# Block ends, store waits, weight fetch and scatter order in a one-core streaming encoder layer

## The reference

```
m = W_out( sigmoid(x Wg_a) * (StickBreak(x) W_oa) + sigmoid(x Wg_b) * (MLA(x) W_ob) )
h = LayerNorm(ALPHA * x + m)
y = LayerNorm(ALPHA * h + PEER(h))
```

## Time and profile before

| what | value |
| --- | --- |
| median of the 3 runs shown | 4035.32 us (4028.1 to 4043.04) |
| profiled execution, own time | 4035.91 us |
| its span (first to last instruction) | 4034.2 us |
| mean granted TensorE clock | 0.883 |
| PE busy | 3200.7 us, 79% of the span |
| DVE busy | 2572.0 us, 64% |
| POOL busy | 1534.7 us, 38% |
| ACT busy | 1130.9 us, 28% |
| DMA | 1097.71 MB, mean 272 GB/s |
| dense stage | from 2486.2 us to the end, 1548 us |

### The profile page before, as it was taken

The page is one execution under the profiler, slowest core; times in us unless marked ns, Lnnn a source line. Parts: engine busy times, 40 slices in busy tenths (PEclk is TensorE's granted clock), DMA queues, the critical chain, the costliest instruction groups (busy, mean ns, idle before and its releaser), DMA issues. The chain is left out here.

```text
span 4034.2 us, 36222 instructions
## 1 busy us (share of the span) xinstructions
PE 3200.7 (79%) x10354; PEld 1799.7 (45%) x10354; DVE 2572.0 (64%) x5114; ACT 1130.9 (28%) x3097; POOL 1534.7 (38%) x1184
## 2 busy tenths in 40 slices
PE   9968998476757679388676593889998999989977
PEld 5735654242534445254354252444444444444433
DVE  0112148685746766575774674688888888888884
ACT  0212122352422522354342331222222222222211
POOL 0000026562631136463654677633333333333330
PEclk9878999688778889698877796999999999999999
DMA  5634479645467889544546696999999999999994
GB/s 159 245 138 132 157 278 350 232 132 161 130 222 268 286 319 335 192 130 140 161 130 201 193 293 205 336 392 404 398 393 409 412 407 405 389 410 398 400 405 138
DMA packets 373897, 1097.71 MB, mean 272 GB/s; under 512 B 90272, under 2 KB 208192, under 8 KB 287552
## 3 DMA queue, kind: packets, MB, share of 16 engines
q0 software_dynamic: 165072, 751.05, 50.0%
q1 hardware_dynamic: 189040, 326.24, 23.1%
q10 hardware_dynamic: 19584, 18.10, 1.3%
HBM read 1031.16 MB, written 63.02 MB: 271 GB/s over the span
## 5 line engine op out<-in xcount | busy, mean ns | idle before, releaser
L417 POOL DMA_INDIRECT expert_rows<-in_experts,picked_index x640 | 771.1, 1205 | 1554.0 <-DVE ff_sum L572 1441.8
L560 DVE SCALAR_TENSOR_TENSOR expert_rows<-expert_rows,h_tile 128x1024 f32<-128x1024 f32 x672 | 820.2, 1220 | 308.1 <-DMA expert_rows<-in_experts,picked_index 276.1
L572 DVE SCALAR_TENSOR_TENSOR ff_sum<-expert_rows,coefficients,ff_sum 128x1024 f32<-128x1024 f32 x672 | 861.4, 1282 | 112.6 <-ACT coefficients L523 111.2
L1719 PE MATMUL dense_act_ps<-dense_hT,key_columns 128*128 128x384 f32 x2048 | 719.5, 508 | 178.8 <-DMA key_columns<-in_key_columns 98.0
L440 POOL DMA_INDIRECT gates_by_expert<-dense_gate,gate_address x384 | 649.9, 1692 | 202.1 <-issue 143.6
L1727 PE MATMUL dense_out_ps<-dense_value_rows,dense_weights 128*128 128x512 f32 x1536 | 688.2, 600 | 24.5 <-DVE dense_weights L1792 24.4
L1719 PEld LDWEIGHTS dense_act_ps<-dense_hT,key_columns 128*128 128x128 f32 x2048 | 398.8, 198 | 515.5 <-DMA key_columns<-in_key_columns 157.7
L809 PE MATMUL proj_ps<-xT,w_in_block 128*128 128x384 f32 (+1 forms) x1392 | 430.0, 473 | 71.7 <-DMA w_in_block<-in_w_in 31.6
L1727 PEld LDWEIGHTS dense_out_ps<-dense_value_rows,dense_weights 128*128 128x128 f32 x1536 | 294.6, 192 | 378.9 <-issue 319.2
L809 PEld LDWEIGHTS proj_ps<-xT,w_in_block 128*128 128x128 f32 x1392 | 271.5, 196 | 229.8 <-issue 44.5
L517 ACT ACTIVATE activated<-dots 128x1 f32<-128x1 f32 (+2 forms) x620 | 122.4, 197 | 733.1 <-DVE expert_rows L560 718.2
(11 more groups left out here) (181 smaller groups left out, 3383.3 us busy)
## 6 DMA issues: line engine op xcount, KB each, us to landing
key_columns<-in_key_columns SPq DMA_DIRECT2D x128, 512.0 KB, 11.3
dense_value_rows<-in_experts SPq DMA_DIRECT2D x128, 512.0 KB, 8.2
w_in_block<-in_w_in SPq DMA_DIRECT2D x20, 2048.0 KB, 12.6
gates_by_expert<-zeros POOLq DMA_DIRECT2D x12, 2048.0 KB, 33.7
wq_head<-in_peer_wq SPq DMA_DIRECT2D x24, 1024.0 KB, 6.7
dense_gates<-gates_by_expert SPq DMA_DIRECT2D x128, 192.0 KB, 9.6
w_out<-in_w_out SPq DMA_DIRECT2D x3, 4096.0 KB, 13.8
expert_rows<-in_experts,picked_index POOLq DMA_INDIRECT x640, 10.1
```

Source lines behind the costliest of these rows:

```text
L417: pool.indirect_dma_start(to, None, self.a["experts"], bass.IndirectOffsetOnAxis(ap=index[:, k:k + 1], axis=0)).then_inc(self.got[p % self ...
L560: dve.scalar_tensor_tensor(place, place, 1.0, self.h[n % 2][:], ALU.mult, ALU.mult, accum_out=self.dots[:, s % TOPK:s % TOPK + 1]).then_in ...
L572: dve.scalar_tensor_tensor(total, self.ring[:, p % self.RING, D:2 * D], self.coef[:, y % TOPK:y % TOPK + 1], total, ALU.mult, ALU.add).the ...
L1719: mm = nc.tensor.matmul(up[it % 2][:, 0:W], keys[it % KB][:, k, :], hTd[:, k, :], start=(k == 0), stop=(k == KC - 1))
```

## The change

Four things are changed.

1. All blocks but the dense one are opened with `nc.Block(no_gpsimd_drain=True)`: the barrier stays, POOL's DRAIN in front of it goes.
2. The waits for stores at the ends of stages go. Their semaphores now live as long as the program, and the wait stands where the data is read or the buffer is written again: SP waits for stored scores at the start of the next `project` and POOL before it loads a tile's scores; `stick_attend` gets an SP stream that waits for the stored keys and values, and its DVE waits for the stored gates before the first output copy; SP waits for the stored MLA keys at the end of `mla_attend`; SP and ACT wait for the stored h rows at the start of `score_experts`, SP for the dense h at its end; in the dense stage ACT waits for stored scores at the start and SP before the first dense gates.
3. `mla_attend` loads the `w_o` tiles of j = 0 and j = 1; the second ring place moves to 4 KB that are free in that stage. `merge` no longer loads those of j = 1.
4. `SHARES` gets a fifth column, the scatters that each stage may take, and other row counts; a scatter's credit is this number spread over the stage's events (at most 90 of them), at most 4 kept.

```diff
@@ Experts
-        ((1, "project"), 50, 1, 7), ((1, "stick"), 16, 4, 5), ((1, "mla_project"), 8, 1, 1), ((1, "mla"), 12, 4, 4),
-        ((1, "merge"), 10, 2, 1), ((1, "norm"), 9, 1, 1), ((1, "scores"), 24, 1, 5),
-        ((2, "project"), 52, 1, 5), ((2, "stick"), 24, 4, 5), ((2, "mla_project"), 9, 1, 2), ((2, "mla"), 20, 4, 4),
-        ((2, "merge"), 10, 2, 2), ((2, "norm"), 9, 1, 1), ((2, "scores"), 25, 1, 5),
-        ((3, "dense"), 1000, 1, 24),
+        ((1, "project"), 46, 1, 7, 10), ((1, "stick"), 18, 4, 5, 36), ((1, "mla_project"), 9, 1, 1, 14), ((1, "mla"), 12, 4, 4, 30),
+        ((1, "merge"), 11, 2, 1, 14), ((1, "norm"), 9, 1, 1, 12), ((1, "scores"), 24, 1, 5, 12),
+        ((2, "project"), 46, 1, 5, 26), ((2, "stick"), 26, 4, 5, 64), ((2, "mla_project"), 10, 1, 2, 30), ((2, "mla"), 22, 4, 4, 56),
+        ((2, "merge"), 11, 2, 2, 24), ((2, "norm"), 11, 1, 1, 20), ((2, "scores"), 23, 1, 5, 20),
+        ((3, "dense"), 1000, 1, 24, 384),
@@ lay_out_loads
-        waiting, free = [], 0.0
-        last = opened[len(GROUPS) - 1] + 90
+        waiting, credit = [], 0.0
+        share = {block: gates / min(len(self.beside[block]), 90) for block, _, _, _, gates in self.SHARES}
         for k, (block, i, e) in enumerate(points):
-            free = min(free + (1.2 * e[2] if e[0] == "rows" else 0.35), 8.0)
-            while waiting and (free >= 1 or k >= last):
-                free -= 1
+            credit += share[block]
+            while waiting and credit >= 1:
+                credit -= 1
                 self.scatter_at.setdefault(key(k), []).append(waiting.pop(0))
+            credit = min(credit, 4.0)
@@ load_scores
+        stores = [(tile, head) for tiles in GROUPS for head in range(HEADS) for tile in tiles].index((t, h))
+        pool.wait_ge(self.m["scores_stored"][stores % SCORE_STAGES], 16 * (stores // SCORE_STAGES + 1))
@@ project and the six other stages of a group
-        block = s.enter_context(nc.Block())
+        block = s.enter_context(nc.Block(no_gpsimd_drain=True))
@@ project, SP
+            wait_for_scores(sp, m, g.n)
...
-            for i in range(4):
-                sp.wait_ge(gate_out[i], 16 * len(g.runs) * len(gates_of) // 4)
-            sp.wait_ge(out_done, 16 * n_out)
@@ stick_attend, a new SP stream; DVE before the first output copy
+            sp.wait_ge(m["out_stored"], 16 * sum(2 * len(x.runs) + 1 + x.sample for x in upto))
...
+                if n == ends[0]:
+                    for i in range(4):
+                        dve.wait_ge(m["gate_stored"][i], 16 * 4 * sum(len(x.runs) for x in upto))
@@ mla_project, SP
-            sp.wait_ge(out_done, 16 * n_out)
+            sp.wait_ge(out_done, 16 * len(g.runs))
@@ mla_attend, SP
-            for x, w in enumerate((a["w_oa"], a["w_ob"])):
-                sp.dma_start(f["w_o"][0][:, x, :, :], w.rearrange("(k p) c -> p k c", p=P)[:, :, 0:P]).then_inc(m["wo0_in"], 16)
+            for j in range(2):
+                for x, w in enumerate((a["w_oa"], a["w_ob"])):
+                    sp.dma_start(f["w_o"][j][:, x, :, :], w.rearrange("(k p) c -> p k c", p=P)[:, :, P * j:P * (j + 1)]).then_inc(m["wo0_in"][j], 16)
...
+            sp.wait_ge(m["mla_stored"], 32 * min(g.n + 1, len(GROUPS) - 1))
@@ first_norm, SP
-            sp.wait_ge(hT_out, 16 * len(dense)) if dense else None
-            for i in range(2):
-                sp.wait_ge(h_out[i], 16 * ((T + 1 - i) // 2))
@@ score_experts, SP; the same two lines at the start of ACT's stream
+            for i in range(2):
+                sp.wait_ge(m["h_stored"][i], 16 * h_stores(g.n + 1, i))
...
-            for i in range(SB):
-                sp.wait_ge(sc_out[i], 16 * (units // SB))
+            sp.wait_ge(m["hT_stored"], 16 * sum(t in DENSE_TILES for tiles in GROUPS[:g.n + 1] for t in tiles))
@@ dense_experts, SP before the first gates; ACT at its start
+                        wait_for_scores(sp, m, len(GROUPS))
...
+            wait_for_scores(act, m, len(GROUPS))
```

More of the change, by code:

```diff
@@ L120, in hybrid_stream_step @@
             f = spaces[g.n]
-            project(nc, mem, a, m, f, g, bg)
-            stick_attend(nc, mem, a, m, f, g, bg)
+            project(nc, mem, a, m, f, g, bg, groups[:g.n])
+            stick_attend(nc, mem, a, m, f, g, bg, groups[:g.n + 1])
             mla_project(nc, mem, a, m, f, g, bg)
@@ L269, in lay_out @@
         self.beside, row, quantum = {}, 0, 0
-        for block, rows, batch, heads in self.SHARES:
+        for block, rows, batch, heads, _ in self.SHARES:
             rows = min(rows, self.n_steps - row)
@@ L662, in unit_of, with wait_for_scores, project @@
         return self.units.index((GATHERED.index(t), t, h))
-def project(nc, mem, a, m, f, g, bg):
+def wait_for_scores(engine, m, groups):
+    units = HEADS * sum(len(tiles) for tiles in GROUPS[:groups])
+    for i in range(SCORE_STAGES):
+        if units:
+            engine.wait_ge(m["scores_stored"][i], 16 * units // SCORE_STAGES)
+def project(nc, mem, a, m, f, g, bg, earlier):
     bg.begin(g.n, "project")
@@ L697, in project @@
         x_in, = sems(nc, s, "x_in", ids=bg.ids)
-        gate_out = sems(nc, s, *[f"gate_out{i}" for i in range(4)], ids=bg.ids)
+        gate_out, gates_before = m["gate_stored"], 16 * 4 * sum(len(x.runs) for x in earlier)
         last_of = {b: max(n for n, e in enumerate(plan) if e[0] == b) for b in range(len(blocks))}
-        block = s.enter_context(nc.Block())
+        block = s.enter_context(nc.Block(no_gpsimd_drain=True))
         @block.sync
@@ L846, in _ @@
                     if n >= 4:
-                        act.wait_ge(gate_out[n % 4], 16 * len(g.runs) * (n // 4))
+                        act.wait_ge(gate_out[n % 4], gates_before + 16 * len(g.runs) * (n // 4))
                     nc.scalar.copy(gate[n % 4][:], src[:, 0:W]).then_inc(copied, 1)
@@ L855, in _, with stick_attend @@
                 bg.act((e + 1) / N)
-def stick_attend(nc, mem, a, m, f, g, bg):
+def stick_attend(nc, mem, a, m, f, g, bg, upto):
     bg.begin(g.n, "stick")
@@ L894, in scores, with _ @@
             return mm
+        @block.sync
+        def _(sp):
+            sp.wait_ge(m["out_stored"], 16 * sum(2 * len(x.runs) + 1 + x.sample for x in upto))
         @block.gpsimd
@@ L1068, in _ @@
                 n_old = 2
-            n_out = len(g.runs)
             sp.wait_ge(normed, len(squares))
@@ L1405, in _, with h_stores @@
                     bg.dve((j + 1) / KC)
+def h_stores(groups, i):
+    return sum((len(tiles) + 1 - i) // 2 for tiles in GROUPS[:groups])
 def first_norm(nc, mem, a, m, f, g, bg):
@@ L1544, in score_experts @@
         wq_in = sems(nc, s, "wq_in_a", "wq_in_b", "wq_in_c", ids=bg.ids)
-        sc_out = sems(nc, s, *[f"scores_out{i}" for i in range(SB)], ids=bg.ids)
+        sc_out, stored = m["scores_stored"], HEADS * sum(len(tiles) for tiles in GROUPS[:g.n]) // SB
         per = 3 if g.sample else 2
         copies = 2 + 2 * g.sample
-        block = s.enter_context(nc.Block())
+        block = s.enter_context(nc.Block(no_gpsimd_drain=True))
         units = HEADS * T
@@ L1610, in _ @@
         def _(act):
+            for i in range(2):
+                act.wait_ge(m["h_stored"][i], 16 * h_stores(g.n + 1, i))
             for h in range(HEADS + 1):
```

56 lines of the change are left out of this document (30 added, 26 removed).

## The result

The changed kernel takes 3886.1 us (median of 4 runs, 3878.1 to 3902.8) against 4031.7: ratio 0.9641, 95% interval 0.9616 to 0.9666. The forecast was 3900, with 3870 to 3935 for the likeliest case. The profiled execution took 3884.8 us with a span of 3883.1, so 151 us have to be found.

What follows compares the result with a forecast made beforehand. Bound: PE busy 79% of the span, idle at block ends while POOL's transfers land and in stage tails; the dense stage is transfer-bound. 116 + 52 - 25 - 7 = 136 us off 4036 gives 3900 us, range 3835 to 3970.

Steps and rivals of the forecast that it cites:

- A: Block ends: without POOL's drain the stretches shrink to the hand-over; 148.2 us less three deductions gives 116 (40 to 148).
- Fills: Stretch at 201.7: next stage's loads start 21 us earlier but beside zero fills; 14 of 21 kept, so -7 us.
- POOL's own issuing: Block ends: POOL's arrival might be held by its queue, leaving 30.3 us of its work; a third taken, -10 us.
- Late gathers: Blocks of groups 2 and 3 beginning with rows: fetches behind scatters land 1.5 to 3 us late; -15 us (0 to -57).
- half-back rival: Block ends of groups 2 and 3: next block's rows wait for transfers under way, 6 to 7 us more; 3947 us, chance 0.22.
- B: Project stages of groups 2 and 3: fewer rows and scatters, gathers issued earlier; gain 52 us (25 to 64).
- C: Twelve rows moved into stick_attend, mla_project, mla_attend, merge and norm cost DVE time there: -25 us (-30 to -10).
- D: Last scores stage and its end gain 51 us, dense start loses 58 to more scatters: -7 us (-29 to +51).
- the ring: Dense start: ring holds 12 keys, 6.3 MB or 16 us at 402 GB/s, so 89 of 105 us of transfer are lost.
- E, F and G: w_o loaded ahead for merge, the granted clock, and the moved store waits: 0 us each.
- rival that the flag does nothing: Block ends: POOL's queue must still be empty before POOL reaches the barrier; 4031 us, chance 0.08.
- the slower one: Block ends: POOL's queue carried over the barrier makes first rows cost 17.6 against 9.0 us; 4103 us, chance 0.05.

Runs made afterwards that it cites:

- e1: Changed kernel with the old row counts and old placing of scatters; no_gpsimd_drain, moved waits and w_o stay: 3909.4 us, ratio 0.9681.
- e5: Changed kernel with the 12 zero fills issued in the first mla_project after its weights landed, instead of in the first stick_attend: 3872.1 us, ratio 0.9601.
- e7: Changed kernel, one scatter per dense event, one route more in third stick_attend and mla_attend, two fewer in last scores, 16 scatters left for dense: 3870.1 us, 0.9592.
- e8: Changed kernel without the w_o tiles of j = 1 loaded in mla_attend; merge loads them again: 3899.8 us in one execution.
- e4: Changed kernel with all blocks opened without no_gpsimd_drain, so POOL's DRAIN is back; moved waits, w_o and new SHARES stay: 4000.1 us, ratio 0.9898.
- e2: Kernel before with only the new row counts and scatter placing; POOL's DRAIN, stage-end waits and w_o as they were: 4008.9 us, ratio 0.9932.
- e6: Changed kernel with last scores stage's scatter share 40 instead of 20 and one scatter per dense event, 36 left for dense: 3857.4 us, ratio 0.9575.

## Why the prediction was right, and where not

- **A, block ends: 116 foreseen, 119 measured,** by errors that cancelled. Removed: 144.4 us (151.7 to 7.3); the prediction had taken all 148.2 off and nothing for the hand-overs and for SP's last store waits. The three deductions came out at 23.1, 0 and 2.2 in e1 in place of 7, 10 and 15. *Fills:* "I take 14 of 21" failed: of the 21 us nothing stayed, and PE waited until 231 instead of "some 220"; with the fills out of the way (e5) the 21 us are kept. *POOL's own issuing:* the sequencer reports at once at the 20 ends while its engine still works; only at the last end of e1, and at two ends of e7, did POOL signal 1.7 to 2.7 us after the others. *Late gathers:* outside the project and dense stages of the changed kernel DVE waits for rows in two places only, 6.2 us at the start of the second mla_attend and 0.3 us in the last scores stage; "at most 5 us" was missed by a little. Five rows of cover do exceed a landing, and the half-back rival had nothing to stand on. The statement that the other stretches have "DMA shares of 0.50 to 0.94" holds for the longer ones shown; the 13.5 us at 913.8 have 0.14, with POOL at work for 6.9 of them, so not all that the DRAIN waited for was landing.
- The rule weighed beside that, of the Trainium skill (DMA: Bandwidth & Descriptors, Queues, rings and completion order), made the gain 10 us where I had taken 14. It had the right sign, yet the trace goes further: SP's queue had 30.7% of the engines beside 68.4% for POOL's, and its issuing was slower as well. By the same section of the Trainium skill an engine takes a whole packet from one queue before it turns to the next. So "about half" would need packets of one size; as the profile counts packets, POOL's are 9.48 MB / 2395 = 4.0 KB and SP's 1.2 KB. Equal turns would then give 3.3 to 1 in bytes; the window has 2.5 to 1, the same side. No run here changed a packet's size.
- **B, project stages: 52 foreseen, 65.6 measured.** The credit of 0.4 for gathers that can be issued earlier was too small: if the rows gave their 25 us, 40.6 us came of scatters worth 67 us of POOL, a share of 0.6. DVE's waits for rows fell by 48.4 us, and both tails went nearly to nothing.
- **C, moved rows: -25 foreseen,** -15 between e1 and the changed kernel (1196.6 to 1211.6), with a spread of some 10.
- **D, the last stages: -7 foreseen, -22.4 measured.** Gain 41.5 (12.2 of the stage, 29.3 of its end) for 51: DVE's share of the tail was 10 as said, but the part of the stage before the tail grew from 100.8 to 110.2 us. There the DMA share rose from 0.92 to 1.01 and PE waits 9.4 us for `sub_keysT` instead of 0.2; that the earlier gathers fill the engines is likely and was not tried. Loss 63.9 for 58. The step that failed is "all that time SP stands before the first dense gates with every later load of keys behind it". SP never came that far: POOL had put 56 scatters in front of the gather that DVE, ACT, PE and then SP needed, a late gather behind scatters, which A had priced at 3 us a block. The sign "PE waiting for keys" was not seen there: PE waits 73.4 us for gelu. The claim on the ring was wrong too: it has 5 places, 2.6 MB or 6.5 us at 402 GB/s, and SP loads keys for 20 iterations before it comes to that wait, held by PE's progress. With 5 places the prediction's own sum would be 105 - 6.5 - 31 = 67.5, so that 58 for 63.9 came of a wrong chain and a wrong ring at about the right price, since both chains end with POOL's piece of scatters.
- **E, F and G: 0 each,** as found: w_o as in e8; PE's busy time is unchanged, although the mean granted clock of the span rose from 0.883 to 0.899; none of the moved store waits is among the long waits of these views. e4 against e2 bounds E, F and G together with the ends that SP had held: 0.9898 against 0.9932, intervals that overlap.

Sum of the measured parts: 144.4 - 19.3 + 65.6 - 17.2 + 41.5 - 63.9 = 151.1 us, the difference of the two spans. They add up by construction, as they cut the same two traces; which cause each part has rests on e1, e2, e4 and the runs behind them. That the forecast was met within 14 us (3900 for 3886) is partly luck: A was 3 too low, B 14, C 8 to 10, and D 15 too high.

The rival that the flag does nothing fell with the first rows of the profile, the slower one with A. Why a single release of 27 us at the fills gives so little is shown by e5; how much of it is the share of the engines and how much SP's slower issuing was not separated.

## What to carry to other kernels

Here a drain taken off a barrier paid in full where the queue behind it held work that was wanted later, and gave the time back where the next stage wanted the same engines or the same queue at once: fills beside weights, a backlog of scatters in front of a gather. Look at what stands in that queue at each barrier, and move or spread it. When two chains hang on the same resource, breaking one shows the other; take away the resource's load, and count it by what the bound engine (here the transfers) failed to do meanwhile.

## What the runs showed of the hardware that was not expected

- SP's issuing slowed while another queue filled the engines: one load of mla_kT took 1.38 us of SP (median of 8, up to 3.1) beside the fills, and 0.59 us without them. The eighth was issued at 214.9 us, 12.3 us behind the first, instead of 4.5.
- Fills and loads did not share evenly at 196 to 232: 68.4% against 30.7% of the engines' time.
- A block end without the DRAIN lets POOL's sequencer run ahead of its engine across the barrier: behind the release of e6's dense stage the engine first works off 7 scatters and 4 gathers of the stage before. The lead has a limit, since POOL signals 2.7 us after the others at the last end of e1; what sets it was not tried.
